# A hybrid decoder layer step: the order of the first up unit, its loads and the last norm's sums changed

## What is computed

```
ada = (silu(c) @ w_ada + b_ada)              # 9 x D conditioning values per sequence
x <- LN(alpha*x + gate0 * 0.5 * SwiGLU_1(x*(1+scale0)+shift0))
x <- LN(alpha*x + gate1 * W_out[attention | convolution](x*(1+scale1)+shift1))
x <- LN(alpha*x + gate2 * 0.5 * SwiGLU_2(x*(1+scale2)+shift2))
SwiGLU(h) = (silu(h @ wg) * (h @ wu)) @ wd   # D -> 2816 -> D
```

## Time and profile before

| | us |
|---|---|
| median of 3 executions | 904.87 |
| lowest and highest | 904.36, 908.85 |
| the profiled execution | 908.24 |
| its span, first to last instruction | 906.4 |
| TensorE busy in the span | 846.1 (93%) |
| VectorE, ScalarE, GpSimd busy | 455.9, 351.0, 267.7 |

### The profile page before, as it was taken

One profiled execution on the slowest core, in us unless ns is written; L12 is line 12 of the kernel. 1 busy time (PEld: TensorE's weight loads), 2 busy tenths in 40 slices (PEclk: granted clock), 3 DMA queues, 4 the chain that ended last, 5 costly groups with the idle time before them and its releaser, 6 DMA issues.

```text
span 906.4 us, 17053 instructions
## 1 busy us (share of the span) xinstructions
PE 846.1 (93%) x6754; PEld 746.7 (82%) x6754; DVE 455.9 (50%) x708; ACT 351.0 (39%) x502; POOL 267.7 (30%) x326
## 2 busy tenths in 40 slices
PE   5699999999999999999987789879999999999997
PEld 3498998988799989988764556537899999999996
DVE  1444333433233466844686776744864444444353
ACT  2323243232222367355443324173573333432230
POOL 2020000000010131999999999800300000000130
PEclk9599999999899999999999899998999999999998
DMA  9967777879955553416998999998525444644421
GB/s 301 353 202 228 255 242 223 263 226 309 331 174 195 168 159 119 163 47 195 346 314 269 365 329 380 348 348 277 170 72 153 149 139 142 198 141 130 161 70 59
DMA packets 182129, 197.44 MB, mean 218 GB/s; under 512 B 11907, under 2 KB 163705, under 8 KB 182053
## 3 DMA queue, kind: packets, MB, share of 16 engines
q1 hardware_dynamic: 175149, 190.04, 64.8%
q10 hardware_dynamic: 6624, 6.33, 2.2%
q0 software_dynamic: 288, 0.14, 0.1%
HBM read 193.67 MB, written 3.17 MB: 217 GB/s over the span
## 4 chain that ended last, share of the span: by engine, by line
PE 76%; DVE 8%; SPq 5%; DMA 5%; ACT 4%; issue 3%; POOL 1%; DVEq 0%; ACTq 0%; POOLq 0%
PE bank L1599 19%; PE bank L1600 18%; PE bank L1601 18%; PE bank L1871 5%; PE bank L1575 3%; SPq L446 3%; PE bank L1896 2%; DMA raw<-in_w_ada 2%; PE bank L1564 1%; DVE wlo L1089 1%; DMA raw<-in_ffn_wg 1%; DVE kT L1371 1%; PE bank L1631 1%; DMA raw<-in_ffn_wu 1%; PE bank L1625 1%
## 5 line engine op out<-in xcount | busy, mean ns | idle before, releaser
L1089 DVE TENSOR_TENSOR wlo<-raw,whi 128x2048 fp32r<-128x2048 f32 (+1 forms) x80 | 183.3, 2292 | 241.9 <-ACT whi L711 241.6
L1599 PE MATMUL bank<-mh,whi 128*128 128x320 f32 x816 | 257.5, 316 | 0.0
L1601 PE MATMUL bank<-mh,wlo 128*128 128x320 f32 x816 | 252.2, 309 | 0.0
L1600 PE MATMUL bank<-ml,whi 128*128 128x320 f32 x816 | 252.2, 309 | 0.0
L711 ACT CAST whi<-raw 128x2048 fp32r<-128x2048 f32 (+1 forms) x80 | 149.0, 1862 | 232.2 <-PE bank L1601 155.2
L1599 PEld LDWEIGHTS bank<-mh,whi 128*128 128x128 f32 x816 | 153.4, 188 | 10.4 <-issue 10.3
L1600 PEld LDWEIGHTS bank<-ml,whi 128*128 128x128 f32 x816 | 153.5, 188 | 0.1
L1601 PEld LDWEIGHTS bank<-mh,wlo 128*128 128x128 f32 x816 | 153.3, 188 | 0.0
L1599 PE MATMUL bank<-hh,whi 128*128 128x320 f32 x352 | 111.3, 316 | 0.0
L1600 PE MATMUL bank<-hl,whi 128*128 128x320 f32 x352 | 109.6, 311 | 0.0
L1601 PE MATMUL bank<-hh,wlo 128*128 128x320 f32 x352 | 109.5, 311 | 0.0
(11 more groups left out here) (270 smaller groups left out, 1142.1 us busy)
## 6 DMA issues: line engine op xcount, KB each, us to landing
araw<-in_w_ada SPq DMA_DIRECT2D x28, 1024.0 KB, 5.2
raw<-in_ffn_wg SPq DMA_DIRECT2D x22, 1024.0 KB, 7.1
raw<-in_ffn_wu SPq DMA_DIRECT2D x22, 1024.0 KB, 7.3
raw<-in_ffn_wd SPq DMA_DIRECT2D x16, 1024.0 KB, 5.5
raw<-in_cache_k SPq DMA_DIRECT2D x64, 256.0 KB, 4.4
raw<-in_cache_v SPq DMA_DIRECT2D x60, 256.0 KB, 5.4
raw<-in_w_in SPq DMA_DIRECT2D x10, 1024.0 KB, 5.2
raw<-in_w_ada SPq DMA_DIRECT2D x8, 1024.0 KB, 12.2
```

The source lines that it names most:

```text
L1089: dve.tensor_tensor(wl(slot_w(phase, u))[:, 0:size], landed(phase, u)[:, 0:size], wh(slot_w(phase, u))[:, 0:size].bitcast(F32), ALU.subtra ...
L1599: pe.matmul(bank[:, b, 0:T], wh(slot)[:, c], h_, start=(start and n == 0), stop=False)
L1600: pe.matmul(bank[:, b, 0:T], wh(slot)[:, c], l_, start=False, stop=False)
L1601: ins = pe.matmul(bank[:, b, 0:T], wl(slot)[:, c], h_, start=False, stop=(stop and n == len(parts) - 1))
```

## The change

- SP issues the page table and the state copy after the down weights instead of ahead of the up stage. In pair 0 both up weights go ahead of the two conditioning weights. The first conditioning weight of the down stage is loaded ahead of the rest of the constants.
- TensorE runs six more 128 x 128 f32 matmuls with the identity (`keep_clock_early`) after the turn in conditioning steps 3 to 6, and six after the last turn; their result is not read.
- Up unit 0 waits for the high part alone, does all matmuls with it, then waits for the low part and does those with it (`first_unit`).
- In the last norm VectorE adds chunk 6 and its square to the two sums, and TensorE's token sums are four instead of six, with both turns behind them.
- The short description also speaks of the last conditioning turn in the down stage.

```diff
@@ SP
-            sp.dma_start(pages[:, :], i["page_table"].rearrange("b n -> (b n)").unsqueeze(0)).then_inc(ld_pages, 16)
-
-            sp.dma_start(o["conv_sample_new"][0, :, 0:ST - DT, :], i["state_conv"][0, :, DT:ST, :]).then_inc(stored, 16)
...
-                        if ffn == 0:
+                        if ffn == 0 and pair_:
                             load_ada(ADA0 + 2 * pair + x, ADA0 + 2 * pair_ + x)
+                    if ffn == 0 and pair_ == 0:
+                        for x in range(2):
+                            load_ada(ADA0 + x, ADA0 + x)
                 up_pairs(sp, body)
 
             load_up(UP1, 0)
             down_weights(0, 2)
+            load_ada(down_ada(0), down_ada(0))
             sp.dma_start(con[:, C_LN:C_N], i["consts"][:, C_LN:C_N]).then_inc(ld_con, 16)
             down_weights(0, 3)
             for u in range(0, DN1[2], 2):
-                load_ada(down_ada(u), down_ada(u))
+                if u:
+                    load_ada(down_ada(u), down_ada(u))
                 for n in DN_LEAD[u // 2]:
                     down_weights(0, n)
+            sp.dma_start(pages[:, :], i["page_table"].rearrange("b n -> (b n)").unsqueeze(0)).then_inc(ld_pages, 16)
+
+            sp.dma_start(o["conv_sample_new"][0, :, 0:ST - DT, :], i["state_conv"][0, :, DT:ST, :]).then_inc(stored, 16)
@@ VectorE, down
+                            if nxt is None and last and cc == 0:
+                                dve.wait_ge(ysum_step, 4 * sub + 4)
+                                dve.wait_ge(y_ready, 8 * sub + 7)
+                                dve.tensor_tensor(tmp[:, 3, :], tmp[:, 3, :], yT[:, 6, :], ALU.add).then_inc(ysum_step, 1)
+                                dve.wait_ge(sqsum_step, 5 * sub + 5)
+                                dve.wait_ge(sq_ready, 8 * sub + 7)
+                                dve.tensor_tensor(tmp[:, 2, :], tmp[:, 2, :], tmp[:, 0, :], ALU.add).then_inc(sqsum_step, 1)
@@ TensorE, start
+            def keep_clock_early(count):
+
+
+                for _ in range(count):
+                    pe.matmul(bank[:, 3, 0:P], ident, ident, start=True, stop=True)
...
+                if 3 <= u < ADA0 - 1:
+                    keep_clock_early(6)
             ada_turn(ADA0 - 1, ADA0 - 1)
+            keep_clock_early(6)
@@ TensorE, up
+            def first_unit(slot, done, w0, ml0):
+
+
+                pe.wait_ge(w_hi, w0 + 1)
+                for q in range(NCH):
+                    pe.wait_ge(ml_ready, ml0 + q + 1)
+                    for cc in range(2):
+                        c = slice(UC * q + P * cc, UC * q + P * cc + P)
+                        pe.matmul(bank[:, cc, 0:T], wh(slot)[:, c], mh[:, q, :], start=q == 0, stop=False)
+                        pe.matmul(bank[:, cc, 0:T], wh(slot)[:, c], ml[:, q, :], start=False, stop=False)
+                pe.wait_ge(w_lo, w0 + 1)
+                for q in range(NCH):
+                    for cc in range(2):
+                        c = slice(UC * q + P * cc, UC * q + P * cc + P)
+                        ins = pe.matmul(bank[:, cc, 0:T], wl(slot)[:, c], mh[:, q, :], start=False, stop=q == NCH - 1)
+                        if q == NCH - 1:
+                            ins.then_inc(done[cc], 1)
...
+                        if pair_ == 0 and x == 0:
+                            first_unit(slot_w(phase, u_), (gr, w_used), phase[0], ml0)
                         pe.wait_ge(w_lo, phase[0] + u + 1)
-                        if pair_ == 0 and x == 0:
-                            products([(cc, slot_w(phase, u_), cc, (gr, w_used)[cc]) for cc in range(2)],
-                                     m_parts(range(NCH)), lambda n: pe.wait_ge(ml_ready, ml0 + n + 1))
@@ TensorE, last norm
-            pe.wait_ge(ysum_step, 12)
-            pe.wait_ge(y_ready, 22)
+            pe.wait_ge(ysum_step, 13)
             token_sums(0, tmp[:, 3, :], 0)
-            pe.wait_ge(sqsum_step, 15)
+            pe.wait_ge(sqsum_step, 16)
             token_sums(3, tmp[:, 2, :], 0)
-            pe.wait_ge(y_ready, 23)
-            token_sums(0, yT[:, 6, :], 1)
+            pe.wait_ge(y_ready, 24)
+            token_sums(0, yT[:, 7, :], 1).then_inc(rest_ready, 1)
+            pe.wait_ge(sq_ready, 24)
+            token_sums(3, tmp[:, 1, :], 1).then_inc(var_ready, 1)
             turn_out(0)
-            pe.wait_ge(sq_ready, 23)
-            token_sums(3, tmp[:, 0, :], 1)
-            pe.wait_ge(y_ready, 24)
-            token_sums(0, yT[:, 7, :], 2).then_inc(rest_ready, 1)
             turn_out(1)
-            pe.wait_ge(sq_ready, 24)
-            token_sums(3, tmp[:, 1, :], 2).then_inc(var_ready, 1)
```

More of the change, by code:

```diff
@@ L2065, in token_sums @@
                     to = bank[:, b + tt, 0:1] if tt < 2 else bank[64 * (tt - 2):64 * (tt - 2) + 64, b + 2, 0:1]
-                    ins = pe.matmul(to, src[:, P * tt:P * tt + P] if tt < 2 else src[:, SEQ:T], lnones[:, 0:1], start=part == 0, stop=part == 2)
+                    ins = pe.matmul(to, src[:, P * tt:P * tt + P] if tt < 2 else src[:, SEQ:T], lnones[:, 0:1], start=part == 0, stop=part == 1)
                 return ins
```

## The result

The changed kernel takes 899.37 us (median of 10, 897.05 to 902.73); the kernel before, in the same comparison, 906.36 (median of 10, 903.63 to 909.15). The ratio is 0.9915, 95% interval 0.9897 to 0.9933: 7.7 us less, within 6.1 to 9.3 (the two medians differ by 7.0). The forecast was 8.0 us less: 896.9 us, range 893.5 to 901.5, against a median of 904.87 for the kernel before. The profiled execution took 899.64 us, its span is 897.9 (906.4 before), so 8.5 us less between two single executions.

The account below looks back on a forecast made before the run. TensorE, busy 93% of the span, was taken as the bound, with gains only at its waits or half clock. Terms 3.5 + 0.8 + 1.9 + 1.8 = 8.0 us gave 896.9 us against 904.87, range 893.5 to 901.5.

Parts of the forecast that it names:

- 3.5 us for not waiting on the low part: First up unit: needing only the high part, it starts at 38.95 instead of 42.47, 3.5 us gained.
- 0.8 us for the copy: Before the first up unit: moving the copy frees its DMA share, so wg0 lands 0.8 us earlier, bounds 0 to 2.1.
- 1.9 us for the clock: First up unit: added matmuls hold full clock, so its first 15 matmuls save 1.9 us, bounds 0 to 1.9.
- Cost of the added matmuls 0: Conditioning steps before the up stage: product, turn and six matmuls (2.9 us) hide under weights arriving each 3.0 us.
- Load orders 0: Pair 0's loads and the down conditioning weight ahead of the constants: later loads stay covered, gain and cost zero.
- The missing turn 0: Between up and down stages: the described turn move has no line in the diff, so nothing is gained.
- 1.8 us for the tail: Last norm: four token sums instead of six bring VectorE's centring earlier; 1.8 us, bounds 1.1 to 2.4.
- Rival 1: Before the first up unit: clock drops once, the six run cold for a place or two; 898.5 us, chance 0.22.
- rival 2: Before the first up unit: clock stays half through all places, unit starts 5.7 us later; 908.8 us, chance 0.06.
- rival 3: Early up units: another wait (unit 1's or 3's weight late) swallows the start, only the tail stays; 903.1 us, chance 0.12.

Follow-up runs that it names:

- e5: The changed kernel with the page table and state copy issued ahead of the up weights again; ratio 0.9891 to the kernel before.
- e10: The changed kernel with twelve added matmuls instead of six at each of the five places; ratio 0.9945 to the kernel before.
- c0_whole: The changed kernel run once more, unaltered, as yardstick of the first experiment group; ratio 0.9905 to the kernel before.
- e9: The changed kernel with pair 0's loads interleaved again (wg, conditioning, wu, conditioning); ratio 0.9894 to the kernel before.
- c1_whole: The changed kernel run again, unaltered, as yardstick of the second experiment group; ratio 0.9915 to the kernel before.
- e1: The changed kernel with unit 0 alone back in the old order, after the low part; ratio 0.9989 to the kernel before.

## Why the prediction was right, step by step

- **3.5 us for not waiting on the low part:** 38.64 against 42.13 with the order alone undone, 3.49. The cover held as worked out: no wait before the second half, ml in time.
- **0.8 us for the copy:** over-sized. The weight landed 0.33 us earlier in the profile, and 0.4 by the means with e5. My step took the distance between a product's start and the next weight's landing for the distance of two landings; the scatter of the loads between executions (0.75 us in the unit's start) is larger than the term. That SP's issuing is hidden was right.
- **1.9 us for the clock:** unit 0 took 7.24 us instead of 9.10, so 1.86; without the added matmuls it took 8.64, so 1.4 of it is theirs in that execution. What I had not said: the term exists only with the first. In the old order they give 0.3. The agreement with 1.9 is in part luck, as it rests on where the clock rose in one execution of the kernel before.
- **Cost of the added matmuls 0:** right at six, 3.7 us at twelve. The round came out at 3.00 us, not 2.9, the very pace of the weights (3.01), so there was no reserve. Two slips cancelled: the 0.61 us of a turn is its duration with the tail (0.47 to the next start), and six matmuls take 1.53 us, not 1.3.
- **Load orders 0:** right for this kernel by sum, but each of the two is the cover of something. Without pair 0's, TensorE waits 0.36 us; without the one ahead of the constants, 3.19 us once the turn is moved. With the turn in its old place no run undoes that one alone; the kernel before had the constants first and no wait for that weight. I had computed unit 1's cover for the new order only and had not priced the old one.
- **The missing turn 0:** the 2.03 us wait is there to the hundredth. Had the diff held what the description says, 2.0 to 4.9 us more would have gone, about 4 by whole times.
- **1.8 us for the tail:** 1.88 in the profile. In seven of the twelve profiles with the new norm part of the turns ran at half clock: 1.1 us to the end of the kernel in six of them, the lower bound that was forecast for that case, and 0.4 in e10, below it.
- **Sum:** 5.69 us at the start (6.2 forecast) and 1.88 at the end are 7.57, against 7.7 (6.1 to 9.3) by the ratio. The span's 8.5 has 0.9 us more, from between the stages and the middle of the kernel, which no step of the change touches. That 8.0 came so near to 7.7 is in part luck: the copy was half a microsecond too large, nothing was put for that stretch, and the interval is wide enough for both. Rival 1 (six at half clock) and rival 2 (all at half clock) did not show in any profile (clock 1.00 from 20 us to the unit's start in all that have the six); of rival 3 up to 1.1 us showed, in one pair of units.

## What to carry to other kernels

Where a unit waits for two versions of an operand, start with the matmuls that need only the earlier one, and then check what the earlier start will meet next: here two load orders that I had priced at nothing keep 0.4 us away and, once the turn is moved, 3.2. Filler matmuls, whose result is not read, gave 1.4 us where real work followed within 1.3 us and 0.3 where TensorE idled for 4.8, and they cost from the point where a round takes longer than the weights' pace. Read the diff, not the description: a named part that the diff lacked was worth about half as much again as the change by whole times.

## What the runs showed of the hardware

The granted clock differed from execution to execution at the same place of the program: behind the same 2.03 us wait between the stages the kernel before had 6.8 us of half clock, the changed one, c0_whole and e9 3.4, and c1_whole, e1 to e5 and e10 none. The executions that took longer also had a lower mean granted clock (correlation -0.6 over the 51 executions of the kernel before beside the experiments). I expect that this is much of the 5 us by which executions of one kernel scatter, but no run isolates it. Terms of 1 to 2 us were therefore read at their place in the trace.

The other surprise is the copy: 352 KB from DRAM to DRAM, 1.0 us at the loads' 348 GB/s, put a load queued behind it back by 0.4 us by the means of the runs, 0.8 at most.
